# First MLP product: two of the four sums of weight blocks by accumulating transfers on Pool's queue

## What is computed

```python
x = x + merged @ w_out[layer]
h2 = rms_norm(x, norm_mlp[layer])
u = jax.nn.relu(h2 @ w_mlp_up[layer])     # (512, 2048) @ (2048, 8192): this product
x = x + (u * u) @ w_mlp_down[layer]
```

## Time and profile before

| | |
|---|---|
| median of 3 runs | 2712.51 us (2711.56 to 2712.75) |
| the profiled execution, its own time | 2712.3 us |
| its span in the profile | 2710.6 us |
| PE busy | 2695.2 us, 99% of the span |
| DVE busy | 1712.9 us, 63% |
| ACT busy | 1179.8 us, 44% |
| POOL busy | 41.1 us, 2% |
| granted TensorE clock, mean | 0.999 |

### The profile page before, as it was taken

The page is one execution under the profiler, slowest core; times in us unless marked ns, Lnnn a source line. Parts: engine busy times, 40 slices in busy tenths (PEclk is TensorE's granted clock), DMA queues, the critical chain, the costliest instruction groups (busy, mean ns, idle before and its releaser), DMA issues.

```text
span 2710.6 us, 44448 instructions
## 1 busy us (share of the span) xinstructions
PE 2695.2 (99%) x15962; PEld 2398.1 (88%) x15962; DVE 1712.9 (63%) x2977; ACT 1179.8 (44%) x1627; POOL 41.1 (2%) x60
## 2 busy tenths in 40 slices
PE   9999999999999999999999999999999999999999
PEld 8999999788888888888899999999998888888887
DVE  4648887677777754434488878787764444444444
ACT  5534433545555552224344444444443334433342
POOL 0000000000000000000000000000000000000000
PEclk9999999999999999999999999999999999999999
DMA  6444434332222244444333443433456565565653
GB/s 249 125 125 125 138 125 131 93 83 77 77 77 81 78 117 140 139 128 153 117 126 130 132 131 124 139 124 127 136 193 218 186 225 200 192 219 189 230 193 116
DMA packets 359572, 386.96 MB, mean 143 GB/s; under 512 B 16464, under 2 KB 274000, under 8 KB 358992
## 3 DMA queue, kind: packets, MB, share of 16 engines
q1 hardware_dynamic: 331936, 347.24, 40.6%
q10 hardware_dynamic: 27568, 38.81, 4.0%
HBM read 348.23 MB, written 37.75 MB: 142 GB/s over the span
## 4 chain that ended last, share of the span: by engine, by line
PE 98%; DVE 1%; ACT 1%; DMA 0%; issue 0%; ACTq 0%; SPq 0%; DVEq 0%
PE job L1693 7%; PE job L1696 7%; PE job L1695 7%; PE scores L2006 2%; PE scores L2010 2%; PE scores L2008 2%; PE job L2008 2%; PE job L2006 2%; PE job L2010 2%; PE job L2033 2%; PE job L2035 2%; PE job L2034 2%; PE scores L2033 2%; PE scores L2034 2%; PE scores L2035 2%; PE heads_out L1793 1%
## 5 line engine op out<-in xcount | busy, mean ns | idle before, releaser
L1630 DVE TENSOR_TENSOR w_lo_d<-raw_d,w_hi_d 128x512 fp32r<-128x512 f32 x256 | 176.3, 690 | 368.9 <-ACT w_hi_d L1066 368.9
L1366 DVE TENSOR_TENSOR lo<-pair,hi 128x1792 fp32r<-128x1792 f32 x142 | 287.2, 2022 | 122.7 <-ACT hi L843 122.7
L843 ACT ACTIVATE hi<-pair 128x1792 fp32r<-128x1792 f32 x142 | 241.5, 1700 | 267.9 <-PE heads_out L2010 118.5
L1066 ACT ACTIVATE w_hi_d<-raw_d 128x512 fp32r<-128x512 f32 x256 | 161.5, 632 | 405.7 <-PE heads_out L2035 202.8
L677 ACT ACTIVATE w_hi<-raw 128x512 fp32r<-128x512 f32 x272 | 171.1, 631 | 363.4 <-PE job L1696 243.5
L1121 DVE TENSOR_TENSOR w_lo<-raw,w_hi 128x512 fp32r<-128x512 f32 x272 | 189.4, 698 | 167.7 <-ACT w_hi L677 166.6
L1693 PE MATMUL job<-a_hi,w_hi 128*128 128x512 f32 x576 | 235.9, 410 | 1.5 <-DVE w_lo L1121 1.5
L1696 PE MATMUL job<-a_hi,w_lo 128*128 128x512 f32 x576 | 225.9, 392 | 0.0
L1695 PE MATMUL job<-a_lo,w_hi 128*128 128x512 f32 x576 | 224.9, 390 | 0.0
L2006 PE MATMUL scores<-h,hi 128*128 128x256 f32 x512 | 146.1, 285 | 4.7 <-DVE h L1562 2.6
L1636 DVE TENSOR_TENSOR u_lo<-u_raw,u_hi 128x2048 fp32r<-128x2048 f32 x64 | 146.2, 2284 | 4.2 <-ACT u_hi L1072 4.2
(11 more groups left out here) (451 smaller groups left out, 7685.5 us busy)
## 6 DMA issues: line engine op xcount, KB each, us to landing
pair<-in_w_mlp_up SPq DMA_DIRECT2D x256, 256.0 KB, 2.9
u_raw<-u_rows SPq DMA_DIRECT2D x64, 1024.0 KB, 5.6
raw_d<-in_w_mlp_down SPq DMA_DIRECT2D x128, 512.0 KB, 6.1
raw<-in_w_in SPq DMA_DIRECT2D x79, 512.0 KB, 4.1
pair<-in_w_gate SPq DMA_DIRECT2D x84, 256.0 KB, 2.9
raw<-in_w_out SPq DMA_DIRECT2D x64, 256.0 KB, 3.3
u_rows<-u_out ACTq DMA_DIRECT2D x32, 512.0 KB, 4.3
raw<-in_w_in SPq DMA_DIRECT2D x24, 344.0 KB, 3.2
```

What stands on the lines that cost most here:

```text
L843: nc.scalar.activation(pair_hi[j % 2], pairs[j][:, :, 1:8], ACT.Copy).then_inc(pair_hi_ready, 1)
L1066: nc.scalar.activation(w_hi_d[:, j % SPLITS], raw_d[:, j // 2, j % 2], ACT.Copy).then_inc(down_hi, 1)
L1366: nc.vector.tensor_tensor(pair_lo[j % 2], pairs[j][:, :, 1:8], pair_hi[j % 2].bitcast(F32), ALU.subtract).then_inc(pair_lo_ready, 1)
L1630: nc.vector.tensor_tensor(w_lo_d[:, j % SPLITS], raw_d[:, j // 2, j % 2], w_hi_d[:, j % SPLITS].bitcast(F32), ALU.subtract).then_inc(down_ ...
```

## The change

SP issues four transfers for a unit in place of two: after each load of blocks it loads one block once more, 128 KB, into block 4 (the contents of block 1) and block 5 (those of block 2). Pool has a new part, `sum_by_dma`: for every unit it waits until all four loads have landed, does a TENSOR_TENSOR of one column (`pool_pause`), and issues two transfers from SBUF to SBUF, each 128 KB, that add block 0 to block 4 and to block 5. DVE's instruction for blocks 4 and 5 is gone in this stage (it stays in the gate stage); its two others wait for the accumulating transfers. The semaphores `back_loaded` and `out_stored` of the second product are dropped, and `x2_loaded` and `x2_stored` count on in their place, with no transfer or instruction changed.

```diff
@@ load_pair (SP)
                     sp.dma_start(pairs[j][:, :, 2 * h:2 * h + 2].rearrange("p k i c -> p k (i c)"),
                                  wu[h, :, 2 * j:2 * j + 2, bass.ds(p * (2 * P), 2 * P)]
                                  ).then_inc(pair_loaded[j], 16)
+                    sp.dma_start(pairs[j][:, :, 4 + h],
+                                 wu[h, :, 2 * j:2 * j + 2, bass.ds(p * (2 * P) + P * (1 - h), P)]
+                                 ).then_inc(pair_loaded[j], 16)
@@ gpsimd
+            def sum_by_dma(p, j):
+
+                t = pairs[j]
+                pool.wait_ge(pair_loaded[j], p * 64 + (8 * GATE_UNITS + 64))
+                at_least(pool, pool_paused, p * 4 + j)
+                pool.tensor_tensor(pool_pause[:, :], one_half[:, :], one_half[:, :], ALU.mult).then_inc(pool_paused, 1)
+                for h in range(2):
+                    pool.dma_start(t[:, :, 4 + h], t[:, :, 0], accum_op=ALU.add).then_inc(pair_summed[j], 16)
+
+            for j in range(4):
+                sum_by_dma(0, j)
+            with pool.Fori(1, PAIRS) as p:
+                for j in range(4):
+                    sum_by_dma(p, j)
@@ vector
-            sum_pair(GU, 0)
-            sum_pair(GU + 1, 1)
+            def sum_up_pair(m, j):
+
+                t = pairs[j]
+                dve.wait_ge(pair_summed[j], m * 8 + (32 - 8 * j))
+                nc.vector.tensor_tensor(t[:, :, 6], t[:, :, 4], t[:, :, 2], ALU.add).then_inc(sums_second, 1)
+                dve.wait_ge(sums_second, m + (GU + 1))
+                nc.vector.tensor_tensor(t[:, :, 7], t[:, :, 6], t[:, :, 3], ALU.add).then_inc(sums_ready, 1)
+
+            sum_up_pair(0, 0)
+            sum_up_pair(1, 1)
...
                     if not (last and m >= 6):
-                        sum_pair(n + 2, (m + 2) % 4)
+                        sum_up_pair(i * 8 + (m + 2), (m + 2) % 4)
@@ second MLP product, the semaphores alone
-                        sp.wait_ge(out_stored[b], 16 * c)
+                        sp.wait_ge(x2_stored[b], 16 * (BLOCKS + c))
...
-                    dve.wait_ge(back_loaded[t], 16 * (c + 1))
+                    dve.wait_ge(x2_loaded[t], 16 * (BLOCKS + c + 1))
```

More of the change, by code:

```diff
@@ L169, in build @@
         one_half = sb("one_half", [P, 1])
+        pool_pause = sb("pool_pause", [P, 1])
         row_min, row_sum, row_inv = sb("row_min", [P, 2]), sb("row_sum", [P, 2]), sb("row_inv", [P, 2])
@@ L337, in build @@
         u_loaded = [sem(f"u_loaded{i}") for i in range(2)]
-        back_loaded = [sem(f"back_loaded{i}") for i in range(TB)]
-        out_stored = [sem(f"out_stored{i}") for i in range(TB)]
+        pair_summed = [sem(f"pair_summed{i}") for i in range(4)]
+        pool_paused = sem("pool_paused")
         (down_hi, down_split, down_used, u_rounded, u_split, last_done, out_ready) = map(
@@ L585, in load_back @@
                     else:
-                        sp.wait_ge(out_stored[b], 16 * c)
+                        sp.wait_ge(x2_stored[b], 16 * (BLOCKS + c))
                     sp.dma_start(out_tok[:, b], x2_rows[P * b:P * (b + 1), S * c:S * (c + 1)]
-                                 ).then_inc(back_loaded[b], 16)
+                                 ).then_inc(x2_loaded[b], 16)
             def down_loads(c, turn):
@@ L1078, in store_out @@
                     t = (b + 2) % TB
-                    act.dma_start(outt[:, t, S * c:S * (c + 1)], out_tok[:, t]).then_inc(out_stored[t], 16)
+                    act.dma_start(outt[:, t, S * c:S * (c + 1)], out_tok[:, t]).then_inc(x2_stored[t], 16)
             def down_turn(c, turn):
@@ L1108, in _ @@
             for b in range(TB):
-                act.wait_ge(out_stored[b], 16 * BLOCKS)
+                act.wait_ge(x2_stored[b], 16 * 2 * BLOCKS)
         @block.vector
@@ L1586, in _ @@
             split_pair(GU + 1, 1)
-            sum_pair(GU + 2, 2)
-            sum_pair(GU + 3, 3)
+            sum_up_pair(2, 2)
+            sum_up_pair(3, 3)
             combine_acts(6)
@@ L1591, in _ @@
             split_acts(6)
-            sum_pair(GU + 4, 0)
+            sum_up_pair(4, 0)
             split_pair(GU + 3, 3)
@@ L1595, in _ @@
             split_acts(7)
-            sum_pair(GU + 5, 1)
+            sum_up_pair(5, 1)
             def up_pairs(i, first=False, last=False):
```

## The result

The changed kernel takes 2754.49 us (median of 4 runs, 2751.42 to 2757.93), the kernel before beside it 2712.63 us (2711.56 to 2714.07). That is 41.9 us more; the ratio is 1.0156, with a 95% interval from 1.0142 to 1.017. The forecast of 2711.1 us was wrong. The time lies inside the range, and the way there is the first rival, which said 2758 us.

The account below looks back on a forecast made before the run. PE was taken as the bound (busy 2695.2 of 2710.6 us), the transfers hidden. The profiled 2712.3 us minus 1.4 at the stage's start is 2710.9, plus 0.2 for the median gives 2711.1 us; 8-in-10 range 2706.5 to 2767.

Parts of the forecast that it names:

- the first rival: Rival 1: transfers come too late, DVE waits ahead of L1606, then PE; 2758 us at X = 12.8; chance 0.21.
- the cover: In the stage's loop, the largest X that costs no time: some 11.6 us, set by the tightest unit, ahead of `combine_early`.
- X: Time from a split's end to the landing of the second accumulating transfer for the same buffer; taken as 10.3 us.
- 43 us for each us: Loop of buffer reuse: each us of X above 11.7 costs 4/12 us a unit, 43 us over 128 units.
- The loads: Four SP transfers after the split: last starts at 1.6 us, lands 2.9 later, 4.7 us in all.
- The one-column instruction: Pool's instruction before its transfers: about 0.2 us alone, 0.5 taken, at most 2.2 (a whole split).
- The issue y: Pool's issue of one accumulating transfer: 1.1 us taken, 2.2 for both; 0.4 below, 2.33 above.
- The landing z: Landing of a unit's second accumulating transfer: 2.9 us taken, from 2.3 up to 4.4.
- Traffic: DMA share in the stage: from 0.40 to 0.56 with the double loads, 0.72 to 0.88 with accumulates; it fits.
- Rival 2: Pool becomes the bound from y = 2.4 on; at y = 3.0 about 2860 us; chance 0.09.
- Rival 3: DVE is held up while Pool writes the transfers, 5.58 us a unit against PE's 5.04: 2780 us; chance 0.06.
- Rival 4: Clock stays up behind one or both pauses at the stage's start: 1.7 or 3.4 us less, down to 2707.7; chance 0.10.

Follow-up runs that it names:

- e1_loads: Changed kernel with the double loads alone; DVE makes all sums itself and Pool issues no accumulating transfers: 2711.72 us against 2712.22 for the kernel before.
- e5_light: Changed kernel with each main load half as large from the fifth unit on, same number of transfers: 2714.79 us against 2712.19 for the kernel before.
- e2_accum: Changed kernel with the accumulating transfers alone, the double loads left out in the loop: 2711.31 us, ratio 0.9996 to the kernel before.
- e8_entry: Kernel before, with double loads and accumulating transfers for units 0 and 4 only: 2709.47 us against 2712.19 for the kernel before.
- e3_copies: Changed kernel with the accumulating transfers made plain copies of the same bytes, no sum formed: 2715.14 us, ratio 1.0012 to the kernel before.
- e10_early: Changed kernel with the first accumulate waiting only for its own two loads, the one-column instruction ahead of each accumulate: 2728.27 us against 2712.29 for the kernel before.
- e9_half: Changed kernel with one accumulating transfer a unit (block 4); DVE sums block 5: 2710.44 us against 2712.29 for the kernel before.
- e6_tiny: Changed kernel with the accumulates on 16 of 128 partitions: 2709.70 us, ratio 0.9991 to the kernel before.
- e6_long: Changed kernel with 16-partition accumulates, double loads issued in halves and four 512-column Pool instructions added: 2773.11 us against 2712.19 for the kernel before.

## Why the prediction was wrong

**The bound and the cover were right.** PE set the time and DVE's saved 86 us were worth nothing beside it. The cover of 11.6 us held within some tenths: no loss up to X = 10.96, 3 to 5 us between 11.15 and 11.50. Above it 43 us for each us fits the two longest chains (47 for a measured 50, 60 for 57).

**The step that failed** is "X = 4.7 + 0.5 + 2.2 + 2.9 = 10.3 us, 1.3 under the cover: hidden". Measured in the changed kernel over the units that waited, from the split's end:

```
                                     taken        measured
loads landed, Pool starts            4.7          6.31
one-column instruction               0.5          0.62
first issue to DVE's sum             2.2 + 2.9    5.88
X                                    10.3        12.80
```

- *The loads, 1.6 us too short.* I let four transfers land like two, after 2.9 us, since their bytes take 2.4 us at a full window's rate. They land after 3.5 and 3.8 us in the median, and Pool waits for the last of the four: in the units that wait this last load is issued 1.97 us after the split (I had 1.6) and lands 4.3 later. Part of it comes from the four loads themselves: in e1_loads, with no accumulates, the last one is there after 5.5 us. The rest comes with the accumulates. e5_light gets 0.9 back with fewer bytes, and e2_accum, with two loads, needs the 4.67 that I had taken for four. This term alone used up the margin of 1.3 us.
- *The one-column instruction* was nearly right in the mean (0.62 to the first issue). Singly it took from 0.18 to 2.06 us, close to the low and high end that I had named.
- *The issue y was right* (1.2 for 1.1). But I added it twice and then a whole landing, while the landings of the earlier trace rows count from the issue's start, and the second issue starts 0.75 us after the first. That error made X longer by 2.2 - 0.75 = 1.4 us and hid most of how wrong z was:
- *The landing z, 5.1 us for 2.9*, is the mean of the second transfer in the units that wait; 0.75 + 5.1 makes up the 5.88 of the table, since DVE starts within 0.03 us. Of it 3.6 us are the transfer's own time (e8_entry), 0.7 more than I took, and 1.5 come with the traffic of the stage. I had named 4.4 as the upper end and said that longer landings would stay within it.

By their shortest times the loads and the second transfer would have fitted: 5.0 + 0.2 + 0.75 + 3.6 = 9.6 us. What the 10.3 us left out is that both landings grow together when loads and accumulates share the DMA engines.

The Trainium skill (DMA: Bandwidth & Descriptors, Anatomy of one DMA — SWDGE (gpsimd) path) gives an estimate of 2.3 us for this landing. For the plain copies of e3_copies the shortest landing, 2.2 us, agrees and the median of 3.8 does not. For an accumulating transfer the runs do not bear it out: 3.1 us at the shortest, 4.4 in the median of the changed kernel. The measurement decides.

**Traffic.** I expected a share of 0.72 to 0.88; it was 0.96. The loads came as worked out (0.60 in e1_loads for 0.56). The accumulates were reckoned by bytes, 0.16 to 0.32, and took more, since the engines spend 281 us on packets that stay small. This bound stands just behind the loop (e10_early).

**Rival 1** gave 2758 us at X = 12.8, through a y of 2.33; the X came true, through the loads and z, so that the nearness of the two numbers is luck. My condition for it named only y and z, and the term that was off most was the loads, which I took as known.

**Rival 2** did not come: two issues take 2.42 us and Pool is busy half of the time. **Rival 3** did not either. The splits, in the view by tile of the changed kernel (count: shortest/median/longest ns, first and last):

```profile
L1385 DVE TENSOR_TENSOR lo<-pair,hi x142: 2011/2019/2041, 197.4 to 2044.6; 128x1792 fp32r<-128x1792 f32 x142
...
L674 POOL TENSOR_TENSOR pool_pause<-one_half x128: 184/185/2056, 1328.9 to 2032.1; 128x1 f32<-128x1 f32 x128
...
L676 POOL DMA_DIRECT2D pair<-pair x256: 1180/1644/2487, 1329.1 to 2033.2; - x128
```

DVE's splits are not held up: they take at most 2.04 us. It is Pool's one-column instruction that stretches, up to 2.06 us. Of the 128 in the trace 26 take over 0.25 us, and 23 of these end within 0.07 us behind the end of a TENSOR_TENSOR of DVE, 20 times a split, as they would if Pool waited for DVE's instruction to end. The rule of the Trainium skill that the prediction cites (SBUF — State Buffer, two separate sides) agrees with this in both halves: the Pool instruction that reads SBUF contends, and issues leave DVE alone.

**Rival 4 came true beside rival 1.** The start gave -0.7 us in the first pause, as worked out, and the clock stayed up behind both; e8_entry puts the whole at -2.7 us where I had -1.4 to -4.8. That the shorter pause keeps the clock up is not shown, though. Behind a first pause of 1.34 us it is at 1.00 in all eight profiles that have one, but in e1_loads it stays up behind a first pause of the old 2.07 us, and in e3_copies it is at half speed behind the shortened second one:

```profile
1376.00:1378.00 2.00, 2.00 (x11) 2.00 (x10) 2.00 (x2) 0.00 (x0) 2.00 (x2) 0.50 0.00 0
```

It may differ from one execution to the next. The 25 times of the kernel before that ran beside e1_loads fall into two groups, 9 of 2710.48 to 2710.98 us and 16 of 2712.10 to 2712.82; they are 1.7 us apart, which is what I worked out for one pause's drop. It need not be the clock: the profiled execution of e8_entry (2711.59 us, where 8 of its 11 took 2709.16 to 2709.68) has it at 1.00 behind both pauses and reaches the stage's first matmul 1.9 us later than the changed kernel. Each profile shows one execution only, so this stays open.

## What to carry to other kernels

Work that moves from a busy engine onto transfers pays with latency: before pricing the work, price the whole loop from the buffer's release to its next use (issues, landing of the last load, the other engine's turn, issue, landing) against the buffers' depth, and take each landing at the traffic after the change. Where most terms have no row, a margin of a tenth is none: here all four came in above what I took, counted as I had added them up. If such a chain is too long by little, start its first link on its own data (e10_early won 26 of 42 us) or move half of the work (e9_half lost nothing).

## What the hardware showed

- An accumulating transfer within SBUF costs the DMA engines three times a copy of the same bytes: 69632 packets and 281 us against 12288 packets and 95 us.
- It lands 3.2 to 3.7 us after the start of its issue with little beside it (e8_entry), and after 4.1 to 4.7 in the median beside the loads of the stage (the copy after 3.8). One of 16 partitions takes 3.4 in e6_tiny and 2.8 in e6_long.
- Pool takes about 1.2 us to issue one, and 0.72 for the copy. Two in a row take 2.42, the second started 0.75 after the first.
- A Pool instruction of one column takes 0.18 us alone and up to 2.06 beside a TENSOR_TENSOR of DVE of 2.02 (23 of the 26 long ones end with such an instruction); DVE's own time does not change.
- Behind the same pause of 2.07 us the granted clock was 0.56 in the kernel before and 1.00 in e1_loads.
